# Layer norm statistics as columns, two more convolution taps on TensorE, and the finest decay level as a sum with ones

## The reference

```python
def conformer_conv_module(h, w_in, b_in, w_dw, b_dw, ln_g, ln_b, w_out, b_out):
    a, gate = jnp.split(h @ w_in + b_in, 2, axis=-1)
    u = a * jax.nn.sigmoid(gate)
    u = depthwise_conv(u, w_dw, taps=31) + b_dw          # per channel, causal
    u = jax.nn.silu(layer_norm(u, ln_g, ln_b))           # mean and variance over the 2048 channels
    return u @ w_out + b_out

# attention, per chunk of 64 tokens, per head (4 heads of 256 key channels):
cum = jnp.cumsum(log_a, axis=2)
scores[i, j] = sum_d q[i, d] * k[j, d] * exp(cum[i, d] - cum[j, d])     # for i >= j
```

## Time and profile before

| | |
|---|---|
| median of 3 runs | 2198.59 us (2196.92 to 2199.18) |
| the profiled execution's own time | 2196.72 us |
| its span, first to last instruction | 2195.0 us |
| granted TensorE clock, mean of the span | 1.000 |
| TensorE matmul busy | 2180.3 us (99%) |
| VectorE busy | 1406.7 us (64%) |
| ScalarE busy | 992.3 us (45%) |
| GpSimd busy | 202.8 us (9%) |
| DMA | 182 GB/s over the span |

### The profile page before, as it was taken

One profiled execution on the slowest core, in us unless ns is written; L12 is line 12 of the kernel. 1 busy time (PEld: TensorE's weight loads), 2 busy tenths in 40 slices (PEclk: granted clock), 3 DMA queues, 4 the chain that ended last, 5 costly groups with the idle time before them and its releaser, 6 DMA issues.

```text
span 2195.0 us, 32555 instructions
## 1 busy us (share of the span) xinstructions
PE 2180.3 (99%) x13040; PEld 1933.0 (88%) x13040; DVE 1406.7 (64%) x1315; ACT 992.3 (45%) x821; POOL 202.8 (9%) x105
## 2 busy tenths in 40 slices
PE   8999999999999999999999999999999999999998
PEld 8999888888888888888888898888888888888887
DVE  6999786555555655556767677675555555555655
ACT  6666554443344433444364444554443344433444
POOL 7999000000000000000000000000000000000000
PEclk9999999999999999999999999999999999999999
DMA  9665456555555565655544435555555555555562
GB/s 248 183 175 168 142 191 224 179 198 187 187 176 202 173 209 178 210 172 187 192 159 154 150 115 196 202 181 194 189 190 192 185 198 176 200 187 188 174 210 77
DMA packets 250044, 400.48 MB, mean 182 GB/s; under 512 B 6407, under 2 KB 72143, under 8 KB 249935
## 3 DMA queue, kind: packets, MB, share of 16 engines
q1 hardware_dynamic: 249406, 398.74, 54.7%
q0 software_dynamic: 352, 0.56, 0.1%
q10 hardware_dynamic: 208, 0.07, 0.0%
HBM read 397.24 MB, written 2.10 MB: 182 GB/s over the span
## 4 chain that ended last, share of the span: by engine, by line
PE 92%; DVE 4%; issue 2%; DVEq 1%; DMA 0%; ACT 0%; SPq 0%; ACTq 0%
PE bank L1263 54%; PE bank L1265 28%; PE bank L1539 4%; DVE bank L928 2%; PE bank L1336 2%; PE bank L1524 1%; PE bank L1601 1%; DVEq L906 0%; PE bank L1350 0%; DMA x_rows<-in_x 0%; DVE bank L922 0%; PE bank L1353 0%; DVE bank L909 0%; PE bank L1471 0%; PE bank L1504 0%
## 5 line engine op out<-in xcount | busy, mean ns | idle before, releaser
L1263 PE MATMUL bank<-x_both,w_hi 128*128 128x512 f32 x3328 | 1155.6, 393 | 0.0
L771 DVE TENSOR_TENSOR w_lo<-raw,w_hi 128x2048 fp32r<-128x2048 f32 x343 | 779.1, 2290 | 527.2 <-ACT w_hi L486 527.0
L486 ACT ACTIVATE w_hi<-raw 128x2048 fp32r<-128x2048 f32 x374 | 707.5, 1910 | 625.9 <-PE bank L1265 599.4
L1265 PE MATMUL bank<-x_both,w_lo 128*128 128x256 f32 x3328 | 927.0, 279 | 0.0
L1263 PEld LDWEIGHTS bank<-x_both,w_hi 128*128 128x128 f32 x3328 | 623.2, 187 | 141.1 <-issue 0.3
L1263 PE MATMUL bank<-h_both,w_hi 128*128 128x512 f32 x1872 | 649.4, 392 | 0.4 <-DVE h_both L972 0.4
L1265 PEld LDWEIGHTS bank<-x_both,w_lo 128*128 128x128 f32 x3328 | 627.0, 188 | 0.1
L1265 PE MATMUL bank<-h_both,w_lo 128*128 128x256 f32 x1872 | 521.4, 279 | 0.0
L1263 PEld LDWEIGHTS bank<-h_both,w_hi 128*128 128x128 f32 x1872 | 350.5, 187 | 79.5 <-issue 0.5
L1265 PEld LDWEIGHTS bank<-h_both,w_lo 128*128 128x128 f32 x1872 | 352.7, 188 | 0.0
L1336 PE MATMUL bank<-x_both,w_hi 128*128 128x256 f32 x960 | 173.2, 283 | 0.0
(11 more groups left out here) (216 smaller groups left out, 1183.2 us busy)
## 6 DMA issues: line engine op xcount, KB each, us to landing
raw<-in_ffn_w_gate_up SPq DMA_DIRECT2D x176, 1024.0 KB, 5.0
raw<-in_ffn_w_down SPq DMA_DIRECT2D x88, 1024.0 KB, 5.1
raw<-in_gla_w_in SPq DMA_DIRECT2D x48, 1024.0 KB, 5.2
raw<-in_conv_w_in SPq DMA_DIRECT2D x32, 1024.0 KB, 6.2
raw<-in_conv_w_out SPq DMA_DIRECT2D x16, 1024.0 KB, 5.2
raw<-in_gla_w_out SPq DMA_DIRECT2D x16, 1024.0 KB, 6.6
x_rows<-in_x SPq DMA_DIRECT2D x4, 512.0 KB, 6.2
out<-out_rows SPq DMA_DIRECT2D x4, 512.0 KB, 3.1
```

The lines of the kernel that those rows point to most:

```text
L486: nc.scalar.activation(w_hi[k][:, :, :], raw[k][:, :, :], ACT.Copy).then_inc(hi_done, 1)
L771: nc.vector.tensor_tensor(w_lo[k][:, :, :], raw[k][:, :, :], w_hi[k][:, :, :].bitcast(F32), ALU.subtract).then_inc(lo_done, 1)
L1263: mm(to, w_hi[k][:, kt, cols], xx[:, :, k0 + kt, :], start=(first and kt == 0), stop=False, skip_group_check=True)
L1265: ins = mm(to[:, 0:T], w_lo[k][:, kt, cols], xx[:, 0, k0 + kt, :], start=False, stop=(last and kt == 3), skip_group_check=True)
```

## The change

1. `LAST_TAPS` becomes (4, 16): two more of tile 15's taps are matmuls with diagonals. VectorE's tile has two steps fewer; the four taps' sum and join_last(0) come two steps earlier.
2. The sums of the layer norm are made as columns: each 128x256 tile is the weights of two matmuls (one for each 128 tokens) with one column of ones; the results lie in 128x2. The shift that was added on VectorE is a column sum too, with a column of fours.
3. Mean, its square, variance, root and reciprocal work on 128x2. Negative mean and rstd then become diagonals (VectorE), and matmuls of ones with them make rows again, each twice, in two banks. The first copy is read by VectorE for tiles 0 to 2 (mean) and 0 and 1 (rstd); the second is copied to SBUF by ScalarE with two Copies that stand ahead of the first Silu, and serves the other tiles.
4. Ten of the fourteen filler matmuls are left out.
5. The last level (s = 1) makes one exponent of 128x1024, exp(cum of the odd token minus cum of the even), multiplies it by q of the odd and k of the even token, and sums over channels with two matmuls of ones against 512 columns.

```diff
-LAST_TAPS = (4, 14)
+LAST_TAPS = (4, 16)
...
+        last_diag += [sb(f"last_diag{18 + j}", [P, P], 95 * K + 512 * j) for j in range(2)]
...
-        y_total, sq_total = bank[:, 0, 0:T], bank[:, 1, 0:T]
+        y_total, sq_total = bank[:, 0, 0:2], bank[:, 1, 0:2]
+        neg_mean_row, rstd_row = [bank[:, b, 0:T] for b in (4, 6)], [bank[:, b, 0:T] for b in (5, 7)]
...
+            nc.gpsimd.memset(four[:, :], 4.0).then_inc(consts, 1)
...
             scalar.wait_ge(var_done, 1)
-            nc.scalar.activation(rstd[:, :], rstd[:, :], ACT.Sqrt, bias=eps[:, 0:1]).then_inc(root_done, 1)
+            nc.scalar.activation(ln_cols[:, 2, :], ln_cols[:, 2, :], ACT.Sqrt, bias=eps[:, 0:1]).then_inc(root_done, 1)
+            scalar.wait_ge(rows_done, 2)
+            nc.scalar.activation(sq_sum[:, :], neg_mean_row[1], ACT.Copy).then_inc(rows_kept, 1)
+            scalar.wait_ge(rows_done, 4)
+            nc.scalar.activation(rstd[:, :], rstd_row[1], ACT.Copy).then_inc(rows_kept, 1)
             for t in range(KT):
                 scalar.wait_ge(z_done, t + 1)
                 nc.scalar.activation(act[:, t, :], act[:, t, :], ACT.Silu, bias=vcol("ln_b", t)).then_inc(xn_done, 1)
...
+                if n == len(LEVELS) - 1:
+                    scalar.wait_ge(lev_diff, 2 * n + 1)
+                    nc.scalar.activation(dec[:, :, 0:P], dec[:, :, 0:P], ACT.Exp, scale=1.0 / GATE_DIV).then_inc(lev_exp, 1)
+                    return
...
-                    if n == JOIN_AT + 4 and last:
+                    if n == JOIN_AT + 2 and last:
                         join_last(0)
...
-            conv_tile(KT // 2 - 1, 1, LAST_TAPS[1], fewer=LAST_TAPS[0], add_at=9, last=True)
+            conv_tile(KT // 2 - 1, 1, LAST_TAPS[1], fewer=LAST_TAPS[0], add_at=7, last=True)
...
+            nm, msq, var, rs = (ln_cols[:, i, :] for i in range(4))
             dve.wait_ge(stat_done, STAT[1] - 1)
+            nc.vector.tensor_scalar(nm, y_total, -1.0 / D, None, ALU.mult).then_inc(mean_done, 1)
             dve.wait_ge(mean_done, 1)
+            nc.vector.tensor_tensor(msq, nm, nm, ALU.mult).then_inc(mean_done, 1)
             dve.wait_ge(mean_done, 2)
             dve.wait_ge(stat_done, STAT[1])
+            nc.vector.scalar_tensor_tensor(out=var, in0=sq_total, scalar=1.0 / D, in1=msq,
                                            op0=ALU.mult, op1=ALU.subtract).then_inc(var_done, 1)
+            for a in range(2):
+                ins = nc.vector.tensor_scalar(neg_mean_diag[:, a * P:(a + 1) * P], ident[:, :], nm[:, a:a + 1], None, ALU.mult)
+            ins.then_inc(mean_diag, 1)
+            dve.wait_ge(root_done, 2)
+            nc.vector.reciprocal(rs, var).then_inc(rstd_done, 1)
+            dve.wait_ge(rstd_done, 2)
+            for a in range(2):
+                ins = nc.vector.tensor_scalar(rstd_diag_ln[:, a * P:(a + 1) * P], ident[:, :], rs[:, a:a + 1], None, ALU.mult)
+            ins.then_inc(ln_diag, 1)
...
+                if t == 0:
+                    dve.wait_ge(rows_done, 3)
+                if t == 2:
+                    dve.wait_ge(rows_kept, 2)
+                nc.vector.scalar_tensor_tensor(out=act[:, t, :], in0=act[:, t, :], scalar=vcol("ln_g", t),
+                                               in1=rstd_row[0] if t < 2 else rstd[:, :],
                                                op0=ALU.mult, op1=ALU.mult).then_inc(z_done, 1)
...
+            def column_sums(to, tile, start=False, stop=False, by=None):
+
+                by = ones[:, 0:1] if by is None else by
+                for a in range(2):
+                    ins = mm(to[:, a:a + 1], tile[:, a * P:(a + 1) * P], by, start=(start and a == 0), stop=stop,
+                             skip_group_check=True)
+                return ins
...
+            pe.wait_ge(consts, 21)
+            column_sums(y_total, shift, start=True, by=four[:, :])
             pe.wait_ge(ysum_done, KT - 1)
-            mm(y_total, ones[:, :], y_sum[:, :], start=True, stop=False)
+            column_sums(y_total, y_sum)
...
-            for signal, count, n in ((var_done, 1, 2), (root_done, 2, 7), (rstd_done, 2, 1), (z_done, 1, 2), (xn_done, KT + 1, 2)):
+            pe.wait_ge(mean_diag, 1)
+            for row in neg_mean_row:
+                mm(row, ones[:, :], neg_mean_diag[:, :], start=True, stop=True).then_inc(rows_done, 1)
+            pe.wait_ge(ln_diag, 1)
+            for row in rstd_row:
+                mm(row, ones[:, :], rstd_diag_ln[:, :], start=True, stop=True).then_inc(rows_done, 1)
+            for signal, count, n in ((z_done, 1, 2), (xn_done, KT + 1, 2)):
...
+                elif n == len(LEVELS) - 1:
+                    e = dec[:, :, 0:P].rearrange("p (h c) (a m) -> p c a h m", c=2, a=2)
+                    to = pair_s[(n + 1) % 2].rearrange("p (a h m) -> p a h m", a=2, h=HEADS)
+                    for kk in range(2):
+                        ins = mm(to, ones[:, :], e[:, kk, :, :, :], start=(kk == 0), stop=(kk == 1))
```

More of the change, by code:

```diff
@@ L141, in trunk @@
         sq_early = sb("sq_early", [P, 8, T], 72 * K)
-        last_diag = [sb(f"last_diag{j}", [P, P], 80 * K + 512 * j) for j in range(sum(LAST_TAPS))]
-        assert sum(LAST_TAPS) <= 18
+        last_diag = [sb(f"last_diag{j}", [P, P], 80 * K + 512 * j) for j in range(18)]
+        last_diag += [sb(f"last_diag{18 + j}", [P, P], 95 * K + 512 * j) for j in range(2)]
+        assert sum(LAST_TAPS) <= len(last_diag)
+        ln_cols = sb("ln_cols", [P, 4, 2], 93 * K)
+        four = sb("four", [P, 1], 93 * K + 64)
+        neg_mean_diag = sb("neg_mean_diag", [P, T], 91 * K)
+        rstd_diag_ln = sb("rstd_diag_ln", [P, T], 92 * K)
         y_sum = sb("y_sum", [P, T], 69 * K)
@@ L229, in trunk @@
         var_done = sem("var_done")
+        mean_diag = sem("mean_diag")
+        ln_diag = sem("ln_diag")
+        rows_done = sem("rows_done")
+        rows_kept = sem("rows_kept")
         cent_done = sem("cent_done")
@@ L967, in _ @@
             ln_center(0)
-            invert(1, rstd[:, :])
+            ln_center(1)
             def ln_remainder(t):
@@ L976, in _ @@
                 dve.wait_ge(cent_done, t + 1)
-                nc.vector.scalar_tensor_tensor(out=act[:, t, :], in0=act[:, t, :], scalar=vcol("ln_g", t), in1=rstd[:, :],
+                if t == 0:
+                    dve.wait_ge(rows_done, 3)
[3 more added lines that the diff above has]
+                                               in1=rstd_row[0] if t < 2 else rstd[:, :],
                                                op0=ALU.mult, op1=ALU.mult).then_inc(z_done, 1)
-                if t + 1 < KT:
+                if 1 <= t + 1 < KT and t + 1 != 1:
                     ln_center(t + 1)
@@ L1119, in halves, with neighbours @@
                 return tile.rearrange("p k (b h r) -> p (k b) h r", h=2, r=s)
+            def neighbours(tile, odd):
+                return tile.rearrange("p k (m b) -> p k m b", b=2)[:, :, :, odd]
             def level_exponents(n):
@@ L1134, in level_operands @@
                 dve.wait_ge(lev_exp, n + 1)
+                if n == len(LEVELS) - 1:
+                    e = dec[:, :, 0:P]
+                    nc.vector.tensor_tensor(e, e, neighbours(q_t, 1), ALU.mult).then_inc(lev_mul, 1)
+                    dve.wait_ge(lev_mul, 2 * n + 1)
+                    nc.vector.tensor_tensor(e, e, neighbours(k_t, 0), ALU.mult).then_inc(lev_mul, 1)
+                    return
                 nc.vector.tensor_tensor(d[:, :, 0, :], d[:, :, 0, :], k[:, :, 0, :], ALU.mult).then_inc(lev_mul, 1)
@@ L1396, in _ @@
             free_slot(0, U_CONV_OUT // 2)
+            def column_sums(to, tile, start=False, stop=False, by=None):
[4 more added lines that the diff above has]
+                return ins
             def add_square(square, signal, count, start=False, stop=False):
                 pe.wait_ge(signal, count)
-                return mm(sq_total, ones[:, :], square, start=start, stop=stop)
+                return column_sums(sq_total, square, start, stop)
             add_square(sq_late[:, 4, :], y_sq, 4, start=True)
             add_square(sq_late[:, 5, :], y_sq, 5)
+            pe.wait_ge(consts, 21)
+            column_sums(y_total, shift, start=True, by=four[:, :])
             pe.wait_ge(ysum_done, KT - 1)
-            mm(y_total, ones[:, :], y_sum[:, :], start=True, stop=False)
+            column_sums(y_total, y_sum)
             for tile in range(2):
@@ L1409, in _ @@
             pe.wait_ge(join_done, KT)
-            mm(y_total, ones[:, :], act[:, KT - 2, :], start=False, stop=False)
+            column_sums(y_total, act[:, KT - 2, :])
             add_square(sq_late[:, 6, :], y_sq, 6)
             pe.wait_ge(join_done, KT + 2)
-            mm(y_total, ones[:, :], act[:, KT - 1, :], start=False, stop=True).then_inc(stat_done, 1)
+            column_sums(y_total, act[:, KT - 1, :], stop=True).then_inc(stat_done, 1)
             add_square(sq_late[:, 7, :], y_sq, 7, stop=True).then_inc(stat_done, 1)
```

(3 more changed lines are left out.)

16 lines of the change are left out of this document (9 added, 7 removed).

## The result

The changed kernel takes 2202.19 us (median of 22 executions, 2199.84 to 2203.89), the kernel before on the same chip 2199.12 (22 executions, 2196.88 to 2202.34). The ratio is 1.0013 [1.0008, 1.0019]: 3 us slower, less than the 0.2% that the prediction took as the least that can be told, but the interval leaves 1 out. The forecast was 2198.3, its range ended at 2201.3. Rival B, the falling clock, had given 2201.8.

The account below looks back on a forecast made before the run. TensorE, busy 2180.3 of 2195.0 us, was taken as the bound. The table load's +1.47 and the last level's -1.79 gave -0.32 us, or 2198.3 against the median 2198.59; range 2195.6 to 2201.3.

Parts of the forecast that it names:

- Rival B: Layer norm, 215 to 226 us: the clock falls to 1.2 GHz, adding 3.5 us, for 2201.8 us; chance 15%.
- the sum: Whole kernel: +1.47 for the table load, -1.79 for the last level, together -0.32 us on a span of 2195.0.
- Part 1: Two more taps on TensorE: VectorE's last join moves from 217.36 to 216.54; two more ScalarE diagonals cost nothing.
- Part 2: Layer norm sums as columns: 0.45 us each, TensorE ends last, mean read at 219.22 (before 218.58).
- Rival C: Layer norm: column sums overlap and cost half, 0.22 us each, mean 1.5 us earlier, for 2196.8 us; chance 7%.
- Part 3: Layer norm's column chain from variance to rows: first tile scaled at 222.10 instead of 222.28, 0.18 us gained.
- Part 4: ScalarE in the norm: table load behind the second Copy, first Silu at 224.27 instead of 222.80, 1.47 us later.
- Rival A: Layer norm: Silu's table load stays hidden behind the root, sum -2.0 us, for 2196.6 us; chance 10%.
- Rival D: Layer norm: ScalarE is held behind the table load for 1.28 us more, for 2199.6 us; chance 3%.
- Part 5: Last attention level: two 512-column matmuls take 1.73 us where 16 matmuls took 3.52, a gain of 1.79 us.

Follow-up runs that it names:

- e4: The changed kernel with a one-column Silu directly behind the square root, so the table loads there; 2197.89 us, ratio 0.9992.
- e9: The changed kernel with its ten fillers put back, two ahead of the mean rows, eight behind the rstd rows; 2201.43 us, ratio 1.0009.
- e2: The changed kernel with the old last level, so only the layer norm part and the two taps changed; 2203.57 us, ratio 1.0021.
- e3: The changed kernel with 64 columns of ones in place of one in the column sums; 2198.36 us, ratio 0.9997.
- e5: The changed kernel with both 64 columns in the sums and a one-column Silu behind the root; 2195.5 us, ratio 0.9986.
- e6: As e5, but with 14 taps of the last tile on TensorE in place of 16; 2196.75 us, ratio 0.9991.
- e10: As e5, but with five fillers in place of two behind the first Silu; 2197.78 us, ratio 0.9990.
- e11: e5 repeated unchanged; 2198.48 us, ratio 0.9990.
- e1: The kernel before with the new last level alone; 2197.58 us, ratio 0.9991.
- e7: The kernel before with 16 taps of the last tile on TensorE in place of 14, nothing else; 2199.06 us, ratio 0.9998.
- e8: The kernel before without ten of its fourteen filler matmuls, sums still as rows; 2201.11 us, ratio 1.0005.
- e12: As e5, but with 16 columns of ones in place of 64; 2198.77 us, ratio 0.9999.

## Why the prediction was wrong, point by point

**Failed: the sum had no term for the clock.** It took the granted clock as 1.00 at 215 to 230 and left the fall to rival B at 15%. The reason for the low chance was "the longest gap of no work at all is about 1.9 us". No gap was needed. From 215.07 to 219.6 TensorE went from one column sum to the next without a pause, and the clock fell at the end of that; it stayed at half for 10.2 us and cost 1.71 + 1.04 = 2.75 us around the norm. By profiles: with one column the clock fell at 219.6, 218.1 (e4) and 217.8 (e9) inside the sums, and at 220.1 (e2), 0.4 behind them; with 16 at 218.4; with 64 not at all in e3, e5 and e6, and after the sums in e10 and e11 (220.8, 221.0); with row sums not at all in the kernel before, e1 and e7, and at 222.2 without fillers (e8). That narrow columns bring the fall forward is shown by e12 against the kernels with 64, in the profiles and in the mean clock of all executions; what in the chip makes the difference is not.
The Trainium skill, TensorE: Matmul & The Clock Gate, section HAM oscillation, warns of long idle gaps between bursts of matmuls. e8 agrees: its TensorE did nothing from 218.9 to 222.7 and the clock fell at 222.2. The prediction took this as covering a merely thinned-out stage, which is wider than what the section says. In the changed kernel the result was as B had it, but not by such a gap: TensorE had none over 216 to 219.

**B's number, in part luck.** Rival B had the place right and its 2201.8 lies within 0.4 us of the median. Its terms were +1.7 for the rows and +1.8 for the product at half clock; measured 1.71 and 1.04. The fall at the gate product, 1.55 in the profiled execution, nobody had put in, and the kernel before came out at 2199.12 in 22 executions where the forecast had built on the 2198.59 of three. The stated range ended at 2201.3, below B's own figure. The profiles of e2, e4, e7, e8, e9, e10 and e12 have a fall at the gate product as well, those of the kernel before, e1, e3, e5, e6 and e11 have none: e7 and e8 have the norm's statistics of before, so it needs no column sums. Whether the change makes it more frequent stays open. Over all executions the mean granted clock was 0.9966 for the changed kernel and 0.9990 to 0.9992 for the kernel before beside the experiments.

**Part 1, right.** Diagonals: 16 in 4.79 us against 14 in 4.19, the copy behind them 0.69 later, almost without a trace at 208 us (taps from 208.27 against 208.14 in the earlier trace rows, and 0.11 of the 0.13 is there already at 115 us, ahead of the diagonals). TensorE ends last, by 2.27 us of VectorE's waiting. The taps gain nothing (e7).

**Part 2, right.** 0.45 us a column sum, one column or 64; the mean was read at 219.40, forecast 219.22. Rival C falls.

**Part 3, right at full clock.** First tile scaled at 222.21 in e3 (forecast 222.10); e5's first product 0.19 earlier than before.

**Part 4, right.** The load begins at 222.96 in e3 (forecast 222.97), the first Silu at 224.25 (224.27), the product at 225.81 (225.91). Rival A falls, and e4 and e5 show what A would have given. Rival D falls: load at 224.77 and Silu at 226.06, 1.29 apart, and 222.96 to 224.25 in e3. The Trainium skill, ScalarE: Activation LUTs, section What ACT_TABLE_LOAD costs, adds a drain of 1.38 us; none shows, and the measurement decides.

**Part 5, right.** 1.72 us in the chain, forecast 1.73; e1 gains 1.9 in the span and 1.65 in the median.

So at full clock the forecast's sum of -0.3 agrees with what was measured: e3, whose clock stayed up in the profile, has a ratio of 0.9997 [0.9988, 1.0006]. Its span is 1.5 above that of before and not 0.3 below; the slower pace of the last section, 1.9 us, makes up the difference.

## What to carry to other kernels

A TensorE that is busy without a pause is no proof that the clock holds: in streams of matmuls with one or 16 columns it fell at a busy share of 100%, with 64 columns it held through the sums. Read the granted clock of the stretch before believing the steps; and where the moving operand can be widened at no cost in time, as from 1 to 64 columns here, try it. An operation that needs no table load of its own, as the Copy here, still holds back the load queued behind it; a one-column call of the next function, placed in the wait before, took the load off the path (e5 and e11, ratios 0.9986 and 0.9990, both intervals below 1). These two are faster than both kernels, but not by more than the level explains: e1, the level alone, has 0.9991. So the norm as columns, mended in both places, is not shown to gain anything over the norm of before.

## What the runs showed of the hardware that was not expected

The clock fell to 1.2 GHz inside an unbroken stream of matmuls (0.79 to 0.90 over 216 to 219 in e9, e4 and e12, TensorE busy for 3.00 of 3.00). A late first product and the low clock may feed each other. The clock rose at 229.9 in the changed kernel, whose product waited for the table, and at 224.9 in e4, whose product did not; in e2, with the late load, it was up at 223.5 and fell again at 226.9, after TensorE had stood still from 224.7 to 226.2. The mean clock of all executions points the same way (0.9966 and 0.9969 with the late load, 0.9978 and 0.9979 with the early one, at one or 16 columns), but no run tests it alone.

At the same granted clock of 1.00 the product after the norm goes at one of two paces. Over 260 to 280 the kernel before has

```profile
260.00:280.00 20.00, 20.00 (x118) 17.62 (x117) 15.92 (x18) 8.32 (x12) 0.00 (x0) 1.00 0.56 199
```

118 matmuls, e3 and e11 have 115. Measured from pair to pair of matmuls that is 0.347 against 0.353 us. From ScalarE's copy at 230 us to its table load at 332 it is 101.78 against 103.69, 1.9 us. e5, e6 and e9 go at the slower pace too, the changed kernel, e10 and the others at the faster. Three of the four kernels with 64 columns have it, and the repeat of e5 has it again, so it may belong to the kernel and be a price of the 64 columns; against that, e9 has it with one column, e10 with 64 has not, and the medians of e3, e5 and e11 are no higher than the sums without it. Whether kernel or execution decides, and its cause, stay open.
